# Moving two thirds of a conditioning product into the common weight stream of a hybrid decoder trunk

## The chip, the cores and the metric

The kernel runs on one core of one Trainium2 chip. The metric is the device time of one execution in microseconds (us). A core has five engines that this text names: PE (TensorE, matmuls, with its weight loads PEld), DVE (VectorE), ACT (ScalarE), POOL (GpSimd) and SP (SyncE, which here only issues DMAs). Each runs its own list of instructions in order and waits on semaphores for the others.

## The reference

All values are float32. With P = 128, D = 1024, 2048 prompt positions and 8 x 8 = 64 sample positions:

```
mod = silu(c) @ w_ada + b_ada                     # (9 conditioning rows) x 1024 x 6144
sh1, sc1, g1, sh2, sc2, g2 = split(mod, 6)
h   = x * (1 + sc1) + sh1
a_b, a_c, a_x, g_u, g_v, p_x = split(h @ w_in)    # 1024 x 2048
y_a = a_b * conv3(a_c * a_x)                      # 256 channels
y_b = g_u * (W_s @ LN(g_v) + b_s)                 # 512 channels, 128 x 128 per head and chunk
y_c = pool_map(trailing_means(p_x) - p_x)         # 256 channels
x   = LN(alpha * x + g1 * (concat(y) @ w_out))
h2  = x * (1 + sc2) + sh2
x   = LN(alpha * x + g2 * (relu(h2 @ w_up)**2 @ w_down))
```

There are 9 conditioning rows: one for the prompt, eight for the sample batch. New convolution, pooling and gating states are outputs too. The change concerns `mod`: only `sh1` and `sc1` are needed before the first projection; `g1`, `sh2`, `sc2` and `g2` are needed later.

## The kernel before, in words

**Precision.** A float32 product of large operands is three matmuls of split operands (`mm3`, lines 844 to 847): each operand is a high part of type fp32r and a low part (value minus high part). A weight slab is 128 x 1024 values (512 KB). SP loads it into one of `RAW = 2` raw buffers (`slab`), ACT copies it to the high part in one of `SLOTS = 4` slots of `w_hilo` (line 744, `hi_part`), and POOL subtracts to make the low part (line 686, `lo_part`). Slab g is loaded once the low part of slab g - 2 is made, and its high part is made once PE is done with slab g - 4. All of `w_in`, `w_out`, `w_up` and `w_down` passes through this one stream.

**Supers.** The prompt is cut in four supers of 512 positions; the fourth also carries the 64 sample positions (tiles `nt == 5`, 576 columns). For each super a mixer runs: four slabs for v (`v_slab`), then the "F phase" of twelve feature-major slabs F0 to F11 (`fm_product`, 24 matmuls each), then eight output slabs (`o_product`). The parts of F0 to F11 are, in order, c x b of the first 128 convolution channels, pool 0, u 0, pool 1, u 1, then c x b of the second half, u 2, u 3. Between them stand S (position mixing of tiles 0, 1 and of 2, 3), M (the pooling map, which waits for the pooled differences `d_ready` from DVE) and, in the first super, B (a bias table). The order is written out by hand in `mixer_stages`, once for PE and once for DVE. After the four mixers comes the MLP, 16 groups per super.

**Banks.** The F slabs of supers 1 and 2 take four PSUM banks in turn, those of the first and the fourth super two.

**The modulation product.** `w_ada` is cut in `N_ADA = 24` pieces of 256 columns (1 MB each). For a piece, SP loads the weights and the bias row (into 9 partitions), PE runs 8 plain float32 matmuls with 9 stationary columns (`ada_product`, line 857), DVE adds the bias (line 1199), PE turns the result in two transposes (`ada_turn`, line 865), DVE copies it to `modT` (lines 1208, 1210), and SP stores the row to `mod_rows`. Eight pieces (`ADA_FIRST`) stand in the opening, between the first transposes of x and the v slabs; the other sixteen stand in the F phase of the first super (`("A", u)`). `g1` and `g2` come back from `mod_rows` by a broadcast load. Two pieces share two banks, so the next product waits for DVE's copy of the last (`ada_T`).

**The opening.** The small tables, the state rows and w_s are loaded before pieces 1 and 2 and the tiles of x.

Of the kernel before, what the change touches and what calls it, by code (L numbers as in the profile page):

```python
# [38 lines left out]
MIX_SLABS = 24  # L39
SLAB_FM, SLAB_O = 4, 16  # L40
# [13 lines left out]
N_ADA = 24  # L54
ADA_COLS = 6 * D // N_ADA
ADA_FIRST = 2 * D // ADA_COLS


def ada_col(u):

    if u < ADA_FIRST:
        return (SH1 if u % 2 else SC1) * D + ADA_COLS * (u // 2)
    return ADA_COLS * u


N_PRE = 3 + 2 + 2 + 1 + 1 + 2 + 1
# [27 lines left out]
def fm_turns(nt, first):  # L94
    return 2 if nt == 5 or first else 4


def fm_bank(f, nt, first):
    return 2 * (f % 2) if nt == 5 or first else f % 4
# [53 lines left out]
def ada_pieces_after(f):  # L153
    return [ADA_FIRST + 2 * f, ADA_FIRST + 2 * f + 1] if f < 4 else [ADA_FIRST + 4 + f]


def mixer_stages(s, vector):


    nt, first = tiles_of(s), s == 0  # L160
    F = [("F", n) for n in range(N_FM)]
    S01, S23 = ("S", [0, 1], 0 if nt == 4 else 1), ("S", [2, 3], 2 if nt == 4 else 3)
    if nt == 5:
        S4 = ("S", [4], 0)
        a = [S4, ("V", 1), F[0], ("V", 1)] if vector else [F[0], S4]
        a += [F[1], F[2]] if not vector else [F[1]]
        a += [S01, ("V", 2)] + ([F[2]] if vector else []) + [S23, F[3], F[4]]
    elif vector or first:
# [16 lines left out]


def decoder_layer_kernel(nc, x_prompt, x_sample, c_prompt, c_sample, state_conv, state_pool,
# [5 lines left out]
    with ctx:  # L193
# [38 lines left out]
        hB = sb("hB", [P, 2, KD, GT + ST], F32R)  # L232
# [20 lines left out]
        siluT = sb("siluT", [P, KD * (1 + NB)])  # L253
        ln_now = (sb("mv", [P, 5, 2]), sb("rstd", [P, 5]), sb("rtmp", [P, 5]))
# [38 lines left out]
        ada_out = [sem(f"ada_out{i}") for i in range(4)]  # L293
# [12 lines left out]
        s_pret = sem("s_pret")  # L306
        bias_in = sem("bias_in")
# [101 lines left out]
        def _(sp):  # L409
            def ada_weights(u):  # L410
                if u >= 3:
                    sp.wait_ge(ada_mm, u - 2 if u < ADA_FIRST else u - 1)
# [27 lines left out]
            sp.dma_start(w_s_rows[:, :].rearrange("p (h j) -> p h j", h=HEADS),  # L440
                         w_s[0].rearrange("h i j -> i h j")).then_inc(s_pre, 16)
            sp.dma_start(htmp[0:NB * CONV_BUF, 0, 0:W_CONV],
                         state_conv[0].rearrange("b r c -> (b r) c")).then_inc(s_pre, 16)
            sp.dma_start(htmp[0:NB * POOL_BUF, 1, 0:W_POOL],
                         state_pool[0].rearrange("b r c -> (b r) c")).then_inc(s_pre, 16)
            for half in range(2):
                sp.dma_start(gate_tab[64 * half:64 * half + 64, :, :],
                             bcast(b_s[0].rearrange("(q two) i -> two q i", two=2)[half], 64)
                             ).then_inc(s_pre, 16)
            for c in range(2):  # L450
                sp.dma_start(convw[:, c, :],
                             conv_w[0, :, P * c:P * c + P].rearrange("w p -> p w")).then_inc(s_pre, 16)
            sp.dma_start(pscale[:, :], pool_scale[0].rearrange("(c p) -> p c", p=P)).then_inc(s_pre, 16)
# [1285 lines left out]
```

## Time and profile before

| | us |
|---|---|
| median of three timed runs | 2272.57 (2272.53 to 2274.78) |
| the profiled execution | 2271.71 |
| its span | 2270.0 |
| PE busy | 2190.1, 96% of the span |
| POOL busy | 984.3, 43% |
| DVE busy | 1325.3, 58% |
| mean granted clock of PE | 0.985 of full speed |

The span is what the profiler saw from the first to the last instruction; 1.7 us of the execution lie around it. In the 40 slices of the page PE is below nine tenths only in the first two and in the last. The spans of the stages are: opening 0 to 80 us, F phase of the first super 80 to 236, F phases of supers 1, 2 and 3 305 to 386, 455 to 536 and 610 to 716, MLP from 774 on.

### The profile page before, as it was taken

The page shows a single profiled execution, that of the slowest core. Times are in us where ns is not written, and L with a number is a line of the kernel's source. Part 1 is how long each engine was busy: PE and PEld are TensorE (multiplying, and loading weights), DVE is VectorE, ACT ScalarE, POOL GpSimd, SP SyncE. Part 2 cuts the span into 40 slices and gives each one's busy share as a digit, 9 for nine tenths or more (in the row PEclk, how much of TensorE's full clock was granted, in tenths as well). Part 3 has the DMA queues.
Part 4 walks back from the last instruction along what each step waited for, and adds up shares of the span by engine and source line. Part 5 has one row for each costly group of instructions (what it writes and reads, how often), then busy time and mean ns, then how long its engine had stood idle before and what let it go on. Part 6 is the DMA issues. An engine that isn't in the chain of part 4 may idle for free.

```text
span 2270.0 us, 26946 instructions
## 1 busy us (share of the span) xinstructions
PE 2190.1 (96%) x10686; PEld 1811.2 (80%) x10686; DVE 1325.3 (58%) x1970; ACT 628.0 (28%) x871; POOL 984.3 (43%) x429
## 2 busy tenths in 40 slices
PE   7989999999999999999999999999999999999995
PEld 3556787887788888888888888888888889999994
DVE  1555568587576733654386664376664466555448
ACT  1201322323212333234232333323234322222221
POOL 3312343433323344444464544465454464444454
PEclk9999999999999999999999999999999999999998
DMA  8535353352333245343333434333433322332221
GB/s 257 164 125 175 140 167 103 102 176 102 117 100 117 75 135 167 107 121 111 101 91 123 149 97 126 93 100 104 150 121 102 116 84 77 126 129 88 75 86 50
DMA packets 262832, 269.37 MB, mean 119 GB/s; under 512 B 13080, under 2 KB 220137, under 8 KB 262706
## 3 DMA queue, kind: packets, MB, share of 16 engines
q1 hardware_dynamic: 262706, 267.64, 37.3%
q8 instruction: 85, 1.39, 0.2%
q14 instruction: 41, 0.34, 0.0%
HBM read 249.78 MB, written 17.81 MB: 118 GB/s over the span
## 4 chain that ended last, share of the span: by engine, by line
PE 64%; DVE 4%; POOL 2%; DMA 1%; issue 0%; ACT 0%; DVEq 0%
PE ps L845 21%; PE ps L846 21%; PE ps L847 21%; POOL acc L711 1%; POOL w_hilo L686 1%; PE ps L978 1%; PE ps L1123 1%; PE ps L1124 1%; DMA w_raw<-in_w_up 1%; DVE xt L1607 0%; DVE htmp L1431 0%; DVE hid L1590 0%; DVE st L1233 0%; DVE hid L1593 0%; DVE xt L1635 0%
## 5 line engine op out<-in xcount | busy, mean ns | idle before, releaser
L686 POOL TENSOR_TENSOR w_hilo<-w_raw,w_hilo 128x1024 fp32r<-128x1024 f32 x352 | 910.8, 2596 | 1251.7 <-ACT w_hilo L744 1251.7
L744 ACT ACTIVATE w_hilo<-w_raw 128x1024 fp32r<-128x1024 f32 x352 | 365.4, 1055 | 1070.2 <-PE ps L847 877.1
L1666 DVE TENSOR_TENSOR acc<-acc,ps 128x512 f32<-128x512 f32 x490 | 330.3, 686 | 212.4 <-PE ps L847 204.8
L845 PE MATMUL ps<-w_hilo,hid 128*128 128x512 f32 x1024 | 399.2, 390 | 1.6 <-DVE acc L1663 1.0
L846 PE MATMUL ps<-w_hilo,hid 128*128 128x512 f32 x1024 | 398.7, 389 | 0.0
L847 PE MATMUL ps<-w_hilo,hid 128*128 128x512 f32 x1024 | 398.4, 389 | 0.0
L845 PE MATMUL ps<-hA,w_hilo 128*128 128x512 f32 (+1 forms) x992 | 373.4, 376 | 8.3 <-DVE acc L1460 4.2
L846 PE MATMUL ps<-hA,w_hilo 128*128 128x512 f32 (+1 forms) x992 | 371.1, 374 | 0.0
L847 PE MATMUL ps<-hA,w_hilo 128*128 128x512 f32 (+1 forms) x992 | 370.7, 374 | 0.0
L1590 DVE CAST hid<-htmp 128x512 fp32r<-128x512 f32 (+1 forms) x128 | 61.6, 481 | 378.9 <-ACT htmp L790 378.2
L845 PE MATMUL ps<-hB,w_hilo 128*128 128x288 f32 (+1 forms) x768 | 250.7, 326 | 0.0
L847 PE MATMUL ps<-hB,w_hilo 128*128 128x288 f32 (+1 forms) x768 | 250.4, 326 | 0.0
L846 PE MATMUL ps<-hB,w_hilo 128*128 128x288 f32 (+1 forms) x768 | 250.3, 326 | 0.0
L845 PEld LDWEIGHTS ps<-w_hilo,hid 128*128 128x128 f32 x1024 | 192.2, 188 | 44.0 <-DVE acc L1663 2.4
L847 PEld LDWEIGHTS ps<-w_hilo,hid 128*128 128x128 f32 x1024 | 192.2, 188 | 40.3
L846 PEld LDWEIGHTS ps<-w_hilo,hid 128*128 128x128 f32 x1024 | 192.2, 188 | 39.0
L845 PEld LDWEIGHTS ps<-hA,w_hilo 128*128 128x128 f32 x992 | 189.0, 191 | 40.2 <-DVE acc L1460 4.5
L847 PEld LDWEIGHTS ps<-hA,w_hilo 128*128 128x128 f32 x992 | 188.8, 190 | 31.8
L846 PEld LDWEIGHTS ps<-hA,w_hilo 128*128 128x128 f32 x992 | 189.1, 191 | 30.8
L788 ACT ACTIVATE htmp<-ps 128x512 f32<-128x512 f32 (+1 forms) x128 | 78.2, 611 | 438.4 <-PE ps L847 438.4
L845 PEld LDWEIGHTS ps<-hB,w_hilo 128*128 128x128 f32 x768 | 144.0, 188 | 10.5
L846 PEld LDWEIGHTS ps<-hB,w_hilo 128*128 128x128 f32 x768 | 144.1, 188 | 10.4
(197 smaller groups left out, 2486.7 us busy)
## 6 DMA issues: line engine op xcount, KB each, us to landing
w_raw<-in_w_up SPq DMA_DIRECT2D x128, 512.0 KB, 4.1
w_raw<-in_w_down SPq DMA_DIRECT2D x128, 512.0 KB, 3.6
w_raw<-in_w_in SPq DMA_DIRECT2D x64, 512.0 KB, 3.8
xt<-in_w_ada SPq DMA_DIRECT2D x22, 1024.0 KB
w_raw<-in_w_out SPq DMA_DIRECT2D x32, 512.0 KB, 3.7
xt<-in_x_prompt SPq DMA_DIRECT2D x16, 512.0 KB, 6.8
x_norm<-xt SPq DMA_DIRECT2D x16, 512.0 KB, 6.4
xt<-x_norm SPq DMA_DIRECT2D x16, 512.0 KB, 6.0
```

The source lines that it names most:

```text
L686: pool.tensor_tensor(W[:, g % SLOTS, 1, :], raw[:, g % RAW, :], W[:, g % SLOTS, 0, :], ALU.subtract).then_inc(lo_done, 1)
L711: pool.tensor_tensor(a, a, rows[:, G2_ROW, :], ALU.mult).then_inc(acc_gated, 1)
L744: act.activation(W[:, g % SLOTS, 0, :], raw[:, g % RAW, :], ACT.Copy).then_inc(hi_done, 1)
L788: act.activation(h, fm_view(2 * i, nt), ACT.Relu).then_inc(s_chain_act, 1)
L845: pe.matmul(out, w_hi, x_hi, start=start, stop=False)
L846: pe.matmul(out, w_hi, x_lo, start=False, stop=False)
L847: return pe.matmul(out, w_lo, x_hi, start=False, stop=stop)
L978: ins = pe.transpose(ps[:, set_banks(e, t)[k // 4], P * (k % 4):P * (k % 4) + P], src[:, P * k:P * k + P], ident[:, :])
L1123: pe.matmul(out, x, w_hi, start=start, stop=False)
L1124: return pe.matmul(out, x, w_lo, start=False, stop=stop)
L1590: signal(dve.tensor_copy(hi, x), s_hid_hi, f + 1)
L1666: dve.tensor_tensor(a, a, src, ALU.add).then_inc(d_evac, 1)
```

## The change

1. **Late slabs.** g1, sh2, sc2 and g2, one for each mixer in this order (`LATE`), no longer use pieces. Each is eight slabs of the common stream (`SLAB_A`, two k-tiles x 512 columns each), so a mixer has 32 slabs, not 24. PE multiplies `silu2` (18 stationary columns: the high parts of the 9 rows and their low parts) with the high and the low part of the slab: 4 matmuls a slab (`late_slab`).
2. **Folds.** After four late slabs DVE copies the 18 rows to `arow` (stage C), PE adds the two halves and the bias with a stacked identity in float32 (`late_turn`, stage T; one matmul for g1 and g2, four small ones for sh2 and sc2), and DVE keeps the result (stage K). g1 and g2 are stored to `mod_rows`.
3. **Order.** The late slabs stand from F5 on: F5 A A F6 A A F7 T M F8 A A M F9 A A F10 T F11. On DVE C0 stands behind the work of F6, C1 behind that of F9.
4. **First super.** Its F slabs now take four banks in turn; B stands directly behind F0, its halves in two banks.
5. **Opening.** c, the bias columns, pieces 0 and 1 and the four tiles of x are loaded first (all in `front`, which lies over hB), then the rest in order of use; the bias is added in turned form from `modb`; the low parts of slabs 0 to 3 are made before POOL's preparation of the tables; the small tables are loaded between slabs 4 and 7.
6. **Residual loads.** The four loads of x for the residual (2 MB) follow slab 21 of 32, where they followed slab 13 of 24 (in the first super: they stood before slab 21 of 24).

```diff
-MIX_SLABS = 24
-SLAB_FM, SLAB_O = 4, 16
+MIX_SLABS = 32
+SLAB_F = [4, 5, 6, 7, 8, 9, 12, 15, 16, 19, 22, 23]
+SLAB_A = [10, 11, 13, 14, 17, 18, 20, 21]
+SLAB_O = 24
-N_ADA = 24
-ADA_COLS = 6 * D // N_ADA
+ADA_COLS = 256
+N_ADA = 2 * D // ADA_COLS
+LATE = [G1, SH2, SC2, G2]
+BOTH = 2 * (1 + NB)
...
-    a += [F[5], F[6], F[7], ("M", 0), F[8], ("M", 1)] + F[9:]
...
+    A = [("A", i) for i in range(8)]
+    if vector:
+        a += [F[5], F[6], ("C", 0), F[7], ("K", 0), ("M", 0), F[8], ("M", 1), F[9], ("C", 1), F[10], ("K", 1), F[11]]
+    else:
+        a += [F[5], A[0], A[1], F[6], A[2], A[3], F[7], ("T", 0), ("M", 0), F[8], A[4], A[5], ("M", 1), F[9],
+              A[6], A[7], F[10], ("T", 1), F[11]]
...
-            lo_part(0)
-            lo_part(1)
+            for g in range(4):
+                lo_part(g)
...
+            def late_slab(s, nt, i):
+                g, bank = MIX_SLABS * s + SLAB_A[i], 6 + i // 4
+                pe.wait_ge(lo_done, g + 1)
...
+                for kk in range(2):
+                    k = 2 * (i % 4) + kk
+                    for part in range(2):
+                        ins = pe.matmul(ps[0:BOTH, bank, :], silu2[:, k, :],
+                                        W[:, g % SLOTS, part, HALF * kk:HALF * kk + HALF],
+                                        start=(k == 0 and part == 0), stop=(k == KD - 1 and part == 1))
+                ins.then_inc(slab_used, 1)
+            def late_turn(u):
+                pe.wait_ge(late_copied, u + 1)
+                pe.wait_ge(late_in, 16 * (u + 1))
...
+                if late_row(u // 2):
+                    ins = pe.matmul(ps[0:1 + NB, bank, :], stack[0:r, :], arow[0:r, :], start=True, stop=True)
+                else:
+                    for q in range(4):
+                        ins = pe.matmul(ps[:, bank, (1 + NB) * q:(1 + NB) * (q + 1)], arow[0:r, P * q:P * q + P],
+                                        stack[0:r, :], start=True, stop=True)
...
+            def late_copy(s, u):
+                dve.wait_ge(slab_used, MIX_SLABS * s + SLAB_A[4 * (u % 2) + 3] + 1)
...
+                signal(dve.tensor_copy(arow[0:BOTH, :], ps[0:BOTH, 6 + u % 2, :]), late_copied, u + 1)
...
                     elif stage[0] == "B":
...
-                            pe.wait_ge(fm_evac, 1)
-                            if half:
-                                pe.wait_ge(bias_kept, 1)
-                            ins = sgu_product(ps[:, 0, :], spl[:, 1, :, :], wsT, P, half)
+                            if half == 0:
+                                pe.wait_ge(fm_evac, 1)
+                            ins = sgu_product(ps[:, 3 * half, :], spl[:, 1, :, :], wsT, P, half)
...
-                    if n == 13:
-                        sp.wait_ge(n_stored, 64 * s)
+                    if n == SLAB_A[7]:
+                        if late_row(s):
+                            late_store(2 * s)
+                        if s:
+                            sp.wait_ge(n_stored, 64 * s)
+                        else:
+                            sp.wait_ge(xs_split, 1)
                         load_residual(s)
```

On PE, in the first super between F5 and F6, before (silu is the conditioning, hA the split input, w_hilo the split slab):

```order
L847 MATMUL ps<-hA,w_hilo 128x512
L857 MATMUL ps<-xt,siluT 9x256 x8
L865 MATMUL ps<-ident,gs 128x9 x2
L845 MATMUL ps<-hA,w_hilo 128x512
L846 MATMUL ps<-hA,w_hilo 128x512
```

and now:

```order
L874 MATMUL ps<-hA,w_hilo 128x512
L1014 MATMUL ps<-w_hilo,silu 18x512 x8
L872 MATMUL ps<-hA,w_hilo 128x512
L873 MATMUL ps<-hA,w_hilo 128x512
L874 MATMUL ps<-hA,w_hilo 128x512
```

The piece of 256 columns (8 program matmuls) and its two transposes have become two slabs of 4 matmuls each.

On DVE, in super 1 from the end of pool 1 (F5) over u 1 (F6) to the work of F7 and M0 (spl holds the pooled differences, hB the mixer's output), before:

```order
L1253 CAST spl<-htmp 128x512
L1254 TENSOR_TENSOR spl<-htmp,spl 128x512
L1460 TENSOR_TENSOR acc<-ps,acc 128x512
L1253 CAST hB<-acc 128x512
L1254 TENSOR_TENSOR hB<-acc,hB 128x512
L1377 COPY htmp<-ps 128x512
L1453 TENSOR_SCALAR acc<-ps,pscale 128x512
```

and now (htmp with 18 rows is `arow`):

```order
L1347 CAST spl<-htmp 128x512
L1348 TENSOR_TENSOR spl<-htmp,spl 128x512
L1554 TENSOR_TENSOR acc<-ps,acc 128x512
L1347 CAST hB<-acc 128x512
L1348 TENSOR_TENSOR hB<-acc,hB 128x512
L1293 COPY htmp<-ps 18x512
L1471 COPY htmp<-ps 128x512
L1303 COPY modT<-ps 128x36
```

C0 (line 1293), for which PE's fold T0 waits, stands behind all of DVE's work for F5 and F6.

On SP, in super 1 from the stores of x_norm to the first output slab, before:

```order
L528 DMA x_norm<-xt 128x1024 x4
L500 DMA w_raw<-in_w_in 128x8x128 x4
L514 DMA xt<-in_x_prompt 128x1024 x4
L500 DMA w_raw<-in_w_in 128x8x128 x2
L500 DMA w_raw<-in_w_out 128x2x512
```

and now:

```order
L500 DMA x_norm<-xt 128x1024 x4
L517 DMA htmp<-in_b_ada 1x512
L472 DMA w_raw<-in_w_ada 128x2x512 x2
L472 DMA w_raw<-in_w_in 128x8x128
L472 DMA w_raw<-in_w_ada 128x2x512 x2
L472 DMA w_raw<-in_w_in 128x8x128 x2
L472 DMA w_raw<-in_w_ada 128x2x512 x2
L472 DMA w_raw<-in_w_in 128x8x128
L472 DMA w_raw<-in_w_ada 128x2x512 x2
L486 DMA xt<-in_x_prompt 128x1024 x4
L472 DMA w_raw<-in_w_in 128x8x128
```

Twelve slabs stand between the stores and the residual loads where four stood, and the residual loads now stand directly ahead of slab 22.

## Rows read from the trace of the kernel before

**Rows 1.** The page: busy us (share of the span) x instructions of each engine
```profile
PE 2190.1 (96%) x10686; PEld 1811.2 (80%) x10686; DVE 1325.3 (58%) x1970; ACT 628.0 (28%) x871; POOL 984.3 (43%) x429
```

**Rows 2.** Stages: length; busy us of PE, PEld, DVE, ACT, POOL; PE clock, DMA share, GB/s
```profile
80.00:236.00 156.00, 142.59 (x647) 88.20 (x646) 82.26 (x163) 16.41 (x17) 34.21 (x14) 0.97 0.47 149
305.00:386.00 81.00, 75.33 (x346) 62.50 (x345) 67.11 (x111) 15.33 (x17) 29.44 (x12) 0.96 0.43 144
610.00:716.00 106.00, 93.70 (x651) 92.27 (x651) 84.23 (x163) 15.45 (x17) 29.55 (x12) 0.92 0.34 116
```

**Rows 3.** PE from 80 to 236 us, by form: busy us, mean ns; idle before, releaser
```profile
L857 PE MATMUL ps<-xt,siluT 128*9 128x256 f32 x256 | 62.0, 399 | 9.2 <-DVE modT L1210 9.2
L865 PE MATMUL ps<-ident,gs 9*128 9x9 f32 x32 | 4.6, 213 | 0.4 <-DVE gs L1199 0.4
```

**Rows 4.** PE in order of time, two pieces: start, us, what [idle before <-releaser]
```profile
141.31 3.62 PE L857 MATMUL ps<-xt,siluT 128*9 128x256 f32 x16
...
150.24 6.36 PE L857 MATMUL ps<-xt,siluT 128*9 128x256 f32 x16 [5.10 <-DVE modT L1210]
```

**Rows 5.** PE in order of time, super 1: starts of F5, F6, F8, M1, F9
```profile
339.44 0.40 PE L845 MATMUL ps<-hA,w_hilo 128*128 128x512 f32 x1
...
344.91 0.39 PE L845 MATMUL ps<-hA,w_hilo 128*128 128x512 f32 x1
...
356.47 0.39 PE L845 MATMUL ps<-hA,w_hilo 128*128 128x512 f32 x1
...
366.24 0.79 PE L845 MATMUL ps<-spl,pwT 128*128 128x512 f32 x1 [4.17 <-DVE spl L1254]
...
367.69 0.63 PE L845 MATMUL ps<-hA,w_hilo 128*128 128x512 f32 x1
```

**Rows 6.** PE's waits, 283 to 774 us: us in total, times, longest
```profile
PE ps L845 <- DVE spl L1254: 11.9, 3, 4.2
...
PE ps L845 <- DVE acc L1460: 4.2, 1, 4.2
```

**Rows 7.** DVE in order of time, super 1: pool 1, then u 1
```profile
355.19 0.17 DVE L1410 COPY acc<-pcarry 128x15 f32<-128x15 f32 x1
...
363.45 2.74 DVE L1254 TENSOR_TENSOR spl<-htmp,spl 128x512 fp32r<-128x512 f32 x1
...
367.41 0.69 DVE L1254 TENSOR_TENSOR hB<-acc,hB 128x512 fp32r<-128x512 f32 x1
```

**Rows 8.** POOL in order of time, the same stretch: low parts of slabs
```profile
346.31 2.77 POOL L686 TENSOR_TENSOR w_hilo<-w_raw,w_hilo 128x1024 fp32r<-128x1024 f32 x1 [5.89 <-ACT w_hilo L744]
...
357.19 2.71 POOL L686 TENSOR_TENSOR w_hilo<-w_raw,w_hilo 128x1024 fp32r<-128x1024 f32 x1 [3.04 <-ACT w_hilo L744]
363.30 2.34 POOL L686 TENSOR_TENSOR w_hilo<-w_raw,w_hilo 128x1024 fp32r<-128x1024 f32 x1 [3.40 <-ACT w_hilo L744]
```

**Rows 9.** Loads of w_raw, 270 to 420 us
```profile
DMA to landing us min/median/max: 3.4/3.8/4.5
```

**Rows 10.** ACT in order of time: a slab's high part
```profile
404.86 1.06 ACT L744 ACTIVATE w_hilo<-w_raw 128x1024 fp32r<-128x1024 f32 x1 [2.54 <-PE ps L847]
```

**Rows 11.** SP in order of time, first super: residual loads and the slab behind them
```profile
235.17 1.78 SPq L514 DMA_DIRECT2D xt<-in_x_prompt  x4
...
237.60 0.45 SPq L500 DMA_DIRECT2D w_raw<-in_w_out  x1
```

**Rows 12.** Loads of w_raw, 230 to 262 us
```profile
DMA to landing us min/median/max: 3.5/4.3/9.3
```

**Rows 13.** PE, first super: start of F0
```profile
79.94 0.39 PE L845 MATMUL ps<-hA,w_hilo 128*128 128x512 f32 x1
```

**Rows 14.** DVE, first super: its copy of F0
```profile
89.66 0.69 DVE L1377 COPY htmp<-ps 128x512 f32<-128x512 f32 x1
```

**Rows 15.** PE in the opening: first piece, first transposes of x
```profile
7.40 6.10 PE L857 MATMUL ps<-xt,siluT 128*9 128x256 f32 x16 [3.18 <-DMA gs<-in_b_ada]
...
28.47 0.33 PE L914 MATMUL ps<-ident,acc 128*128 128x128 f32 x1 [3.08 <-DMA xs<-in_x_prompt]
```

More of the change, by code:

```diff
@@ L91, in chunks, with fm_turns, fm_bank @@
     return [(0, GT)] if nt == 4 else [(0, (GT + ST) // 2), ((GT + ST) // 2, GT + ST)]
[L94 to L99, printed above, removed]
+def fm_turns(nt):
+    return 4 if nt == 4 else 2
+def fm_bank(f, nt):
+    return f % 4 if nt == 4 else 2 * (f % 2)
 def v_order(nt):
@@ L167, in mixer_stages @@
         a += [S01, ("V", 2)] + ([F[2]] if vector else []) + [S23, F[3], F[4]]
-    elif vector or first:
+    elif first:
+        a = [F[0], ("B", 0), F[1], S01, ("V", 2), F[2], S23, F[3], F[4]]
+    elif vector:
         a = [F[0], F[1], S01, ("V", 2), F[2], S23, F[3], F[4]]
@@ L292, in decoder_layer_kernel @@
         ada_T = sem("ada_T")
-        ada_out = [sem(f"ada_out{i}") for i in range(4)]
+        late_in = sem("late_in")
+        late_copied = sem("late_copied")
+        late_fold = sem("late_fold")
+        late_kept = sem("late_kept")
+        late_out = sem("late_out")
+        s_silu2 = sem("s_silu2")
+        s_modb = sem("s_modb")
+        st_pre = sem("st_pre")
+        xs_in = sem("xs_in")
         x0_tr = sem("x0_tr")
@@ L446, in _ @@
[L446 to L453, printed above, removed]
@@ new lines, in _ @@
+            ada_weights(1)
+            for t in range(4):
+                sp.dma_start(x0_tile[t], x_prompt[0, P * t:P * t + P, :]).then_inc(x0_loaded, 16)
+            slab(0, free=False)
+            ada_weights(2)
+            ada_weights(3)
+            slab(1, free=False)
+            sp.dma_start(w_s_rows.rearrange("p (h j) -> p h j", h=HEADS),
+                         w_s[0].rearrange("h i j -> i h j")).then_inc(w_s_in, 16)
+            ada_weights(4)
+            slab(2)
+            ada_weights(5)
@@ new lines, in _ @@
+            slab(4)
+            sp.dma_start(g1row[:, 0:W_GMLP], bcast(sgu_b[0], P)).then_inc(bias_in, 16)
+            for half in range(2):
+                sp.dma_start(gate_tab[64 * half:64 * half + 64, :, :],
+                             bcast(b_s[0].rearrange("(q two) i -> two q i", two=2)[half], 64)
+                             ).then_inc(s_pre, 16)
+            slab(5)
+            for c in range(2):
+                sp.dma_start(convw[:, c, :],
+                             conv_w[0, :, P * c:P * c + P].rearrange("w p -> p w")).then_inc(s_pre, 16)
@@ L720, in _ @@
             gate_after = [up_slab(min(MLP_GROUPS * (s + 1) + 1, ALL_GROUPS - 1)) + 1 for s in range(SUPERS)]
-            for g in range(2, N_SLABS):
+            for g in range(4, N_SLABS):
                 lo_part(g)
@@ L990, in mixer @@
                         f = stage[1]
-                        turns = fm_turns(nt, first)
+                        turns = fm_turns(nt)
                         if f >= turns:
@@ new lines, in w_s_turned @@
+            def w_s_turned():
+                dve.wait_ge(s_prepe, 1)
+                dve.wait_ge(s_prep, 1)
+                for half in range(2):
+                    ins = dve.tensor_copy(prep[:, 1, HALF * half:HALF * half + HALF], ps[:, 2 * half, :])
+                    if half:
+                        ins.then_inc(s_pret, 1)
+                    else:
+                        do(ins)
+            ada_copy(0)
+            for n in range(4):
+                ada_copy(2 * n + 1)
+                ada_turned(2 * n)
+                ada_turned(2 * n + 1)
```

427 lines of the change are left out of this document (222 added, 205 removed).

## The prediction

> **What bounds the kernel now.** I read the page's busy table, then the stages, then PE's instruction groups and waits in the F phases, then PE, DVE, POOL and SP in order of time there. PE is busy for 96% of the span, POOL for 43%, DVE for 58% [rows 1]. So PE's own work and PE's waits make the time. The averages hide one thing: in the F phase of super 1 DVE is busy 67.1 of 81.0 us [rows 2], and PE waits there for DVE, 4.17 us before M1 [rows 5]; the same wait makes most of the 11.9 us in three waits of the later mixers, and 4.2 us in the last super [rows 6]. In the F phase DVE runs well behind PE and is nearly as long as PE. The MLP, two thirds of the time, is not touched.
>
> **What goes.** In the first super PE runs 16 pieces. They show as 256 rows, since a float32 matmul shows as two, 62.0 us, with 4.6 us of transposes and 9.2 us of waits for DVE's copies [rows 3]. One wait of 5.10 us is followed by a piece of 6.36 us where others take 3.62 [rows 4]: after such a wait PE runs at half pace (1.2 GHz for 2.4) for some us, which costs 2.7 us here. In super 1 M1's matmuls after the 4.17 us wait show 0.79 us and F9's first 0.63 where others show 0.39 [rows 5]; I put that loss at 2.3, a little under the 2.7 of the longer wait, and 1.7 in the last super.
>
> **What comes on PE.** A slab of 24 matmuls takes 344.91 - 339.44 = 5.47 us, 0.228 each [rows 5]. A late slab is 4 matmuls over 512 columns; the trace has none with 18 stationary columns. I take 0.228 too (9 or 128 stationary columns move at one pace per pass in it): 0.91 a slab, 7.3 for eight, 29.2 for 32. From below it could be nothing cheaper than half (0.45 a slab), from above the float32 pace of rows 4, 3.62/8 = 0.45 for 256 columns, so 3.6 a slab. The folds are float32: 512 columns cost twice a piece's matmul, 0.9 us; the four small ones some 0.6. Eight folds: about 6 us.
> The Trainium skill, "TensorE: Matmul & The Clock Gate", back-to-back issue gap, gives about 131 ns per matmul of 512 columns in a stream. By it the 32 late slabs would cost an estimated 17 us. Rows 5 show 0.228 us, so I stay with 29.2.
>
> **The supply.** A late slab uses PE for 0.91 us but costs the stream as much as any other. With two raw buffers one slab needs 3.8 us of load [rows 9], 1.06 of high part [rows 10] and 2.4 of low part [rows 8], 7.3 us for two slabs in flight, so 3.7 us per slab. F slabs use 5.47. Where F5 ends, four slabs are ready or nearly so; the pattern F A A uses three slabs in 7.3 us and needs 11. Step by step from the end of F5 (344.9, call it 0): low parts of slabs 13, 14, 15, 16 end at 3.7, 6.3, 11.2, 13.8. PE gets to F7 (slab 15) at 9.2 and waits 2 us. Slab 22 stands behind 2 MB of residual loads: at 237.60 such a slab landed 9.3 us after its issue [rows 11, 12], so it would be ready at 41.4, where PE would come at 34 if nothing else held it: a wait of 7.4.
>
> **DVE holds it first.** T0 waits for C0, and C0 stands behind pool 1 and u 1. In the trace DVE starts pool 1 at 355.19, 10.3 us after the end of F5, and ends u 1 at 367.41 + 0.69 = 368.1 [rows 7], 23.2 after it. PE reaches T0 at 1.8 + 5.5 + 1.8 + 2 + 5.5 = 16.6. So T0 waits 23.2 + 0.7 (the copy) - 16.6 = 7.3 us even if DVE is no slower than now. But it is slower: the subtraction of line 1254 takes 2.74 us at 363.45, under POOL's low part of 363.30, and 0.69 at 367.41 without one [rows 7, 8]. DVE's operations on SBUF stand still while POOL works, 2.05 us here. From 344.9 to 368.1 there are four low parts (346.31, one more, 357.19, 363.30) [rows 8]; with the packed stream there are seven (slabs 13 to 19). Three more at 2.05 put C0 at about 30 and the wait at 13. Lower bound 7.3, upper 15. I take 12, nearer to the collisions that rows show each time. Then the clock falls: 2.5 us.
> The rule that speaks against this change: the Trainium skill, "GPSIMD Engine Reference", specifications, says that GpSimd's SBUF interface is shared with VectorE and contended by instructions with two SBUF inputs or in a two-port mode. By that rule, the trace agrees (2.74 against 0.69).
>
> Behind a T0 that late, slab 20 can be made only after F8 (slot of slab 16), and slab 22 only after slab 20: 20.6 us after C0, where PE comes at 19: 1.8 us of wait. The residual loads are hidden then.
>
> **The sum** (against the profiled execution, 2271.7; the median of the runs is 0.9 above).
> Supers 1 and 2: PE's F phase of 81.0 [rows 2] loses the M1 wait, 4.2, and its clock, 2.3; gains late slabs 7.3, folds 1.5, F7 2, T0 12, clock 2.5, F10 1.8: +20.6 each. Bounds: +15 (T0 7.3, but then slab 22 makes PE wait again) and +24.
> Super 3, F slabs longer by an eighth: 106.0 loses 4.2 and 1.7 of clock, gains 7.3, 1.8, 1, 12, 2.5, 0.5: +19; the sparser stream makes it +17. Bounds +9 and +20.
> First super: the work left is 12 x 5.47 = 65.6, S and its short waits 7.5 (what super 1's 81.0 leaves after its slabs, M 1.4, and the 6.5 above), M 1.4, B 2.0, late slabs 7.3, folds 1.8: 85.6. Waits: the pieces covered DVE's norm; its copy of F0 starts at 89.66, 9.7 after F0 starts at 79.94 [rows 13, 14], and B now stands directly behind F0's 5.5, so it waits 5. S01 then stands directly behind F1 and waits some 3 for DVE's convolution. F7 2, T0 11, F10 2, and three falls of the clock 7.5: 30.5. Total 116 against 156.0 [rows 2]: -40. Bounds -49 and -36.
> Opening: PE starts the first piece at 7.40 and the transposes of x only at 28.47, both behind loads, and small tables stand between them [rows 15]. With large loads alone in front I put x at 16 and the pieces never more than 2 us late; PE then needs 8 x 3.6 + 4 x 5.5 + 6 and ends near 71.5 for 79.94: -8. Bounds -12 (no wait for pieces 2 and 3) and -3 (each of the three loads waited for there comes 1.5 to 2 us later).
> Costed at nothing: C1, K0, K1, the small stores and bias loads. DVE's slack from F8 on covers them; without it, 0.7 each.
> Sum: -40 + 2 x 20.6 + 17 - 8 = +10; with T0 at 13 in all, +14. I take +12: 2284 for the profiled execution, 2285 as a median.
>
> **Rivals.**
> A, faster: POOL's packed low parts do not lengthen DVE's chain (they fall on PSUM reads, which rows do not show slowed), T0 waits 7, and slab 22 behind the residual loads is the second wait: -49 + 2 x 15 + 9 - 8 = -18: 2254. For it: 7.3 is all that present times give. Against it: rows 7. The sign turns where the four T0 waits average 9 us rather than 12.
> B, slower: both bounds together, T0 15, and slab 22 late as well: -36 + 48 + 20 - 3 = +29: 2301. For it: each lock loss delays the next low part too.
> C, no saving, the change doesn't do what it says: 18 columns with split slabs run at the float32 pace. 32 x 2.7 = 86 more, 40 of it in T0's waits: 2331. Against it: fp32r slabs on the moving side run at 0.228 in the v slabs.
> D, even: gain in the first super and loss in the others cancel: 2272.
>
> **How the numbers follow.** Forecast (2277 to 2296) 0.47, A 0.27, B 0.15, C 0.02, D 0.09. A measurement tells 0.2%, 4.5 us, from no change. Of A 0.23 are faster and 0.04 the same; of D 0.08 the same and 0.01 slower; B and C are slower; of the forecast's mechanism 0.44 are slower, and 0.03 fall under its range, 0.02 faster and 0.01 the same, by an opening or a first super better than taken. Faster 0.25, same 0.13, slower 0.62. The range is 2256 to 2301; the forecast's own is 2277 to 2296.
>
> **What would show it.** Right: T0's first matmul in each super idle about 12 us behind DVE's copy of 18 rows; C0 about 30 us after F5's end; DVE's SBUF operations from F5 to C0 at 2 to 3 us each; M1 without a wait; the first super's F phase near 116, the others near 102, 102 and 123; F0 starting near 71.5. Wrong: T0 idle 7 us or less with F10 idle over 5 (A); late matmuls above 0.3 us (C); an opening that ends after 77; a second wait in F10 over 4 beside a long T0 (B).

## The result: 1.07% slower, and the profile after

The changed kernel takes 2297.8 us (median of 5 runs, 2293.59 to 2299.83), the kernel before 2272.76 in the same comparison (5 runs). The ratio is 1.0107, 95% interval 1.0096 to 1.0119. The forecast was 2285. The profiled execution took 2293.59 us, 21.9 more than the 2271.7 of before; it is the lowest of the five, and where the other 3 us of the median stand no profile shows.

The page of the profile after, to be held against [rows 1]:
```profile
span 2291.9 us, 26787 instructions
...
PE 2176.9 (95%) x10567; PEld 1812.8 (79%) x10567; DVE 1373.9 (60%) x1959; ACT 660.5 (29%) x903; POOL 1068.1 (47%) x465
```
PE is busy 13 us less than before and the span is 22 us longer: PE's waits grew by 35 us. DVE is busy 49 us more and POOL 84.

The stages, with the columns of [rows 2]: the F phases of supers 0 to 3, and the MLP with the tail.
```profile
75.00:194.00 119.00, 95.08 (x392) 72.67 (x391) 89.14 (x132) 23.89 (x25) 51.74 (x21) 0.89 0.37 115
263.00:367.00 104.00, 86.92 (x391) 68.61 (x390) 81.39 (x115) 22.59 (x23) 47.61 (x19) 0.92 0.46 146
436.00:543.00 107.00, 89.84 (x395) 70.60 (x394) 83.73 (x118) 23.64 (x24) 50.77 (x20) 0.90 0.45 145
617.00:735.00 118.00, 101.96 (x686) 93.84 (x685) 92.63 (x167) 22.58 (x23) 44.64 (x19) 0.94 0.41 131
793.00:2291.00 1498.00, 1468.66 (x7158) 1247.45 (x7156) 847.43 (x1119) 453.47 (x612) 729.13 (x278) 0.99 0.35 109
```
In super 1 DVE is busy 81 of 104 us where it was 67 of 81, and POOL 48 where it was 29. PE's granted clock, 0.96 before, is 0.92: 2.4 GHz for most of the time and 1.2 in stretches behind waits.

PE's waits up to 800 us, to be held against [rows 6] and the 9.2 us of [rows 3]:
```profile
PE ps L1030 <- DVE htmp L1293: 22.9, 2, 11.6
PE ps L872 <- POOL w_hilo L711: 16.1, 8, 3.1
PE ps L1027 <- DVE htmp L1293: 12.4, 2, 7.9
PE ps L872 <- DVE acc L1418: 10.0, 7, 5.5
PE ps L872 <- DVE htmp L1471: 6.3, 1, 6.3
```
L1030 and L1027 are the two forms of the fold T0, and L1293 is DVE's copy C0. The four waits at T0 make 35.3 us, the largest new item. POOL's line is F7, F10 and short ones; the last two lines are S01 and B, mostly in the first super.

PE in order of time in super 1, with the columns of [rows 5] (F5 ends where the first late pair starts):
```profile
303.65 2.00 PE L1014 MATMUL ps<-w_hilo,silu 128*18 128x512 f32 x8
310.97 2.03 PE L1014 MATMUL ps<-w_hilo,silu 128*18 128x512 f32 x8
315.44 0.77 PE L872 MATMUL ps<-hA,w_hilo 128*128 128x512 f32 x1 [2.44 <-POOL w_hilo L711]
...
334.06 1.87 PE L1030 MATMUL ps<-stack,htmp 19*128 19x9 f32 x8 [11.57 <-DVE htmp L1293]
335.86 0.79 PE L872 MATMUL ps<-spl,pwT 128*128 128x512 f32 x1
...
337.31 0.63 PE L872 MATMUL ps<-hA,w_hilo 128*128 128x512 f32 x1
...
355.10 0.47 PE L872 MATMUL ps<-hA,w_hilo 128*128 128x512 f32 x1 [1.57 <-POOL w_hilo L711]
```
In order: A0 A1, A2 A3, F7 behind a wait, T0 behind 11.57 us, M0 and F8 still at 0.63 to 0.79 a matmul where 0.39 is full pace, and F10. A late pair costs 1.85 us (F6 starts at 305.50), 0.93 a slab.

DVE and POOL in the same stretch, against [rows 7, 8]: a step of pool 1 under a low part, the ends of pool 1 and of u 1, and C0; then POOL's first and seventh low part.
```profile
323.69 2.71 DVE L1523 TENSOR_TENSOR acc<-acc 128x512 f32<-128x512 f32 x1
328.67 2.71 DVE L1348 TENSOR_TENSOR spl<-htmp,spl 128x512 fp32r<-128x512 f32 x1
332.60 0.69 DVE L1348 TENSOR_TENSOR hB<-acc,hB 128x512 fp32r<-128x512 f32 x1
333.32 0.68 DVE L1293 COPY htmp<-ps 18x512 f32<-18x512 f32 x1
```
```profile
305.05 2.78 POOL L711 TENSOR_TENSOR w_hilo<-w_raw,w_hilo 128x1024 fp32r<-128x1024 f32 x1 [5.88 <-ACT w_hilo L769]
...
328.27 2.55 POOL L711 TENSOR_TENSOR w_hilo<-w_raw,w_hilo 128x1024 fp32r<-128x1024 f32 x1 [2.42 <-ACT w_hilo L769]
```
C0 starts 333.32 - 303.65 = 29.7 us after F5's end, where u 1 ended 23.2 after it before. That is the forecast step.

In the last super T0 waits less. F5 ends at 675.54, C0 starts 23.7 us behind it, with six low parts between them for the seven of super 1. PE, then DVE:
```profile
700.00 1.26 PE L1027 MATMUL ps<-htmp,stack 19*9 19x512 f32 x2 [4.58 <-DVE htmp L1293]
```
```profile
699.26 0.68 DVE L1293 COPY htmp<-ps 18x512 f32<-18x512 f32 x1
```

Where the 21.9 us are, by the starts and ends of the phases (the last line is read from PE at the start of the MLP):

| | before | after | change | forecast |
|---|---|---|---|---|
| F0 starts | 79.94 | 75.38 | -4.6 | -8 |
| F phase, super 0 | 155.6 | 118.9 | -36.7 | -40 |
| super 1 | 81.1 | 104.1 | +23.0 | +20.6 |
| super 2 | 81.2 | 106.6 | +25.4 | +20.6 |
| super 3 | 105.6 | 117.9 | +12.3 | +17 |
| MLP and tail | 1496.1 | 1498.7 | +2.6 | 0 |

In the first super T0 waits 7.85 us, C0 24.6 us behind F5's end (157.69 - 133.13). Seven low parts stand there too, but DVE is less far behind PE. PE's T0, then DVE's first operation for pool 0 in super 0 and in super 1:
```profile
158.42 1.87 PE L1027 MATMUL ps<-htmp,stack 19*9 19x512 f32 x2 [7.85 <-DVE htmp L1293]
```
```profile
124.47 1.62 DVE L1504 COPY acc<-pcarry 128x15 f32<-128x15 f32 x1
303.12 0.18 DVE L1504 COPY acc<-pcarry 128x15 f32<-128x15 f32 x1
```
That is 8.7 us ahead of F5's end in super 0 and 0.5 in super 1 (F5 ends at 303.65).

### The profile page after: what moved, and what is told of

Read it like the earlier page. It is cut to its first block, busy times and chain, and to the rows that moved or that the text cites. A ratio compares the mean times of both kernels' runs of the same rounds, so it can differ in the third digit from the quotient of the medians.

```text
span 2291.9 us, 26787 instructions
## 1 busy us (share of the span) xinstructions
PE 2176.9 (95%) x10567; PEld 1812.8 (79%) x10567; DVE 1373.9 (60%) x1959; ACT 660.5 (29%) x903; POOL 1068.1 (47%) x465
## 4 chain that ended last, share of the span: by engine, by line
PE 63%; DVE 5%; POOL 2%; DMA 1%; issue 0%; ACT 0%; DVEq 0%; ACTq 0%
PE ps L872 21%; PE ps L873 20%; PE ps L874 20%; DVE xt L1711 1%; POOL acc L736 1%; POOL w_hilo L711 1%; PE ps L1049 1%; PE ps L1198 1%; PE ps L1199 1%; DVE hid L1697 0%; DMA w_raw<-in_w_up 0%; DVE hid L1694 0%; DVE htmp L1525 0%; DVE st L1327 0%; DVE acc L1519 0%
## 5 line engine op out<-in xcount | busy, mean ns | idle before, releaser
L711 POOL TENSOR_TENSOR w_hilo<-w_raw,w_hilo 128x1024 fp32r<-128x1024 f32 x384 | 993.9, 2597 | 1189.2 <-ACT w_hilo L769 1189.1
L769 ACT ACTIVATE w_hilo<-w_raw 128x1024 fp32r<-128x1024 f32 x384 | 398.4, 1054 | 1065.0 <-PE ps L874 715.8
```

The source lines that it names most:

```text
L711: pool.tensor_tensor(W[:, g % SLOTS, 1, :], raw[:, g % RAW, :], W[:, g % SLOTS, 0, :], ALU.subtract).then_inc(lo_done, 1)
L769: act.activation(W[:, g % SLOTS, 0, :], raw[:, g % RAW, :], ACT.Copy).then_inc(hi_done, 1)
```

## The experiments

All are timed against the kernel before on the same chip, 4 to 10 runs each. Each edit is to the changed kernel, unless the text says otherwise. This table has F0's start, the four F phases and the start of the MLP of each profiled run, and the median with the ratio to before.

| | F0 | F phases | MLP | us | ratio (95%) |
|---|---|---|---|---|---|
| after | 75.4 | 118.9 104.1 106.6 117.9 | 793.2 | 2297.8 | 1.0107 (1.0096 to 1.0119) |
| C0 early | 75.7 | 116.8 94.0 94.2 119.9 | 771.0 | 2273.5 | 1.0007 (0.9998 to 1.0016) |
| T0 late | 75.8 | 122.8 95.9 100.4 129.6 | 795.0 | 2293.4 | 1.0088 (1.0070 to 1.0106) |
| small low parts | 75.9 | 108.9 93.9 93.0 114.6 | 756.7 | 2257.9 | 0.9942 (0.9925 to 0.9959) |
| residual late | 76.4 | 117.5 106.7 105.5 119.4 | 800.6 | 2301.1 | 1.0132 (1.0116 to 1.0148) |
| C0 early, residual late | 75.4 | 112.9 98.4 98.9 112.7 | 770.8 | 2274.1 | 1.0008 (0.9999 to 1.0018) |
| and C1 early | 75.2 | 112.2 90.5 90.4 112.9 | 765.3 | 2261.8 | 0.9940 (0.9926 to 0.9953) |
| B behind F1 | 75.4 | 108.1 105.3 105.6 119.1 | 784.0 | 2285.7 | 1.0058 (1.0045 to 1.0070) |
| opening | 73.8 | 117.2 107.9 105.5 116.4 | 791.2 | 2294.5 | 1.0094 (1.0080 to 1.0107) |
| all of these | 72.5 | 102.9 92.6 94.6 113.0 | 749.9 | 2248.0 | 0.9889 (0.9876 to 0.9903) |
| and the store | 72.1 | 102.4 92.3 94.5 113.1 | 746.7 | 2248.8 | 0.9890 (0.9875 to 0.9906) |
| and late slabs spread | 72.4 | 97.8 93.5 94.1 120.4 | 749.8 | 2251.9 | 0.9909 (0.9893 to 0.9924) |

### Is it the place of C0? Its copy early
```diff
-        a += [F[5], F[6], ("C", 0), F[7], ("K", 0), ("M", 0), F[8], ("M", 1), F[9], ("C", 1), F[10], ("K", 1), F[11]]
+        a += [F[5], F[6]]
+        a.insert(-1 if nt == 5 else -2, ("C", 0))
+        a += [F[7], ("K", 0), ("M", 0), F[8], ("M", 1), F[9], ("C", 1), F[10], ("K", 1), F[11]]
```


> Only VectorE's order changes: its copy of the first 18-row half (C0) stands ahead of pool 1 in supers 0 to 2, and behind pool 1 but ahead of u 1 in the last. Theory (T0 waits because C0 stands behind 13 to 30 us of VectorE's chain): the four waits at T0 of 7.9, 11.6, 11.3 and 4.6 us go nearly to 0, and the clock's loss behind them (1.5 each) with them, about -40. F8 then comes sooner, and slab 22, behind 2 MB of residual loads, is late: F10's wait grows from 1.9 to some 8 in supers 0 to 2, +18. Sum about -22: 2275. Rival (the packed stream is the limit, T0 only the first to show it): PE waits as long at F8, M1 or F9; 2292 to 2299.

Measured 2273.5: 24 us less than the changed kernel, at the expected figure. In super 1 T0 stands at 319.11 directly behind F7 with no wait. The wait that comes instead in super 0 is F10's, the slab behind the residual loads (PE in order of time):
```profile
178.49 0.77 PE L874 MATMUL ps<-hA,w_hilo 128*128 128x512 f32 x1 [9.64 <-POOL w_hilo L713]
```
In the last super F10 waits 6.05. In super 1 it is M1, 3.42 us behind pool 1 at 331.77. The place of one copy of 0.68 us is worth the whole net loss against before.

### Is it DVE held by POOL? Small low parts
```diff
+                n = P if g < MLP0 and g % MIX_SLABS in SLAB_A else D
-                pool.tensor_tensor(W[:, g % SLOTS, 1, :], raw[:, g % RAW, :], W[:, g % SLOTS, 0, :],
+                pool.tensor_tensor(W[:, g % SLOTS, 1, 0:n], raw[:, g % RAW, 0:n], W[:, g % SLOTS, 0, 0:n],
```


> Leaves out seven eighths of the low part of the 32 late slabs: GpSimd's subtraction for them is 128x128 for 128x1024 (PE still multiplies all of it, with old numbers in the rest). Theory (each low part holds VectorE's SBUF operations for 2.05 us): C0 in super 1 ends about 24 us after F5's end and not 30.4, so T0 waits some 5 for 11.6; F7's waits of 2.4 go too. Supers 0 to 2: -9 each, the last -4, with clock about -30: 2268. Rival (GpSimd's work does not lengthen VectorE's chain): T0's waits stay within 1 us of 11.6 plus what F7 gives back, total -2 to -6: 2292 to 2296.

Measured 2257.9, 40 us less than the changed kernel, more than expected. Its page:
```profile
PE 2170.8 (96%) x10567; PEld 1809.7 (80%) x10567; DVE 1309.6 (58%) x1959; ACT 661.1 (29%) x903; POOL 1004.8 (45%) x465
```
DVE has the same 1959 instructions and not one of them was changed, and it is busy 1373.9 - 1309.6 = 64.3 us less: 2.0 us for each of the 32 low parts. POOL is busy 63.3 us less. That the two agree this closely proves little: in the other runs of this section, whose low parts are whole, DVE is busy 1362.3 to 1375.5 us, so that a low part is worth 1.6 to 2.1. In super 1 F5 ends at 294.16, and on DVE
```profile
313.89 0.68 DVE L1294 COPY htmp<-ps 18x512 f32<-18x512 f32 x1
```
C0 stands 19.7 us behind it and not 29.7: five times 2.0, and two whole low parts are left there where seven stood. T0 waits 4.73. Not all of the 40 us is DVE's: the slabs come sooner too, and F7 waits 1.10, 0.70 and 0.78 us in supers 0 to 2 where it waited 2.4. The rule of the Trainium skill, "GPSIMD Engine Reference", specifications (an SBUF interface shared with VectorE), is borne out by this, with its price beside it.

### Are the residual loads hidden? They alone late
```diff
-                        load_residual(s)
...
+                    if SLAB_F[11] <= n < SLAB_F[11] + 4:
+                        load_residual(s, [n - SLAB_F[11]])
```


> Only SyncE's order changes: the four residual tiles are loaded one by one behind slabs 23 to 26 instead of all together between slabs 21 and 22. Theory (hidden behind the long T0): F10's waits of 1.9 stay, since slab 22 waits for slab 20 and that for F8's slot; no change within 3 us, 2295 to 2300. Rival (slab 22 is late by its load): F10's waits go, -2 and some clock in three supers, about -9: 2289.

Measured 2301.1, 3 more than the changed kernel, with intervals that touch. F10 still waits 1.9 to 2.1 us in supers 0 to 2. Beside a long T0 the loads cost nothing where they stand, as forecast; late, they seem to cost a few us in the output phases (the MLP starts 7.4 us later, of which F0 and the F phases make 2.6).

### With T0 out of the way: both edits, then C1 too


> Both edits, VectorE's early C0 and the residual tiles behind slabs 23 to 26. Theory: the waits at T0 go and slab 22 does not take their place: -40 in all, 2258; F phases near 105, 91, 93 and 112. Rival (stream packed two late slabs to one F slab is the limit): no more than 3 us better than the early C0 alone.

Measured 2274.1, the same as with C0 early alone. The theory's 2258 was wrong and the rival's figure came, but not by its mechanism. F10's long wait in super 0 falls from 9.6 to 3.8 (112.9 for 116.8), but in super 1 the next fold, T1, takes its place (in the last super 7 us are gained, in supers 1 and 2 4.4 and 4.7 lost). PE, then DVE:
```profile
345.98 0.38 PE L1033 MATMUL ps<-stack,htmp 19*128 19x9 f32 x1 [4.78 <-DVE htmp L1296]
```
```profile
345.24 0.68 DVE L1296 COPY htmp<-ps 18x512 f32<-18x512 f32 x1
```
DVE runs without a gap from F5's end at 297.70 to this copy C1. Its order has C1 behind pool out 1 and the b copy, so the fold once more stands where PE meets the end of DVE's chain. The next run moves C1 ahead of both:
```diff
-        a += [F[7], ("K", 0), ("M", 0), F[8], ("M", 1), F[9], ("C", 1), F[10], ("K", 1), F[11]]
+        a += [F[7], ("K", 0), ("M", 0), F[8], ("C", 1), ("M", 1), F[9], F[10], ("K", 1), F[11]]
```


> Early C0 and late residual tiles as in the run before, and C1 ahead of pool out 1 and the b copy on VectorE. Theory (VectorE is now the longer chain, and each fold is a point where PE meets its end): T1's waits of 4.8 and 4.0 in supers 1 and 2 go, with 1.5 of clock each; part of it comes back as waits for hB ahead of the output products. Total -7: 2267. Rival (VectorE busy without a gap to the end of the mixer, so that whatever is moved PE waits for its end): within 2 us of 2274.

Measured 2261.8, 12 less, where 7 were expected. T1 stands at 340.22 behind F10 with no wait and supers 1 and 2 take 90.5. This is faster than before by 0.6%.

### The same on PE's side: T0 behind M1
```diff
-        a += [F[5], F[6], ("C", 0), F[7], ("K", 0), ("M", 0), F[8], ("M", 1), F[9], ("C", 1), F[10], ("K", 1), F[11]]
+        a += [F[5], F[6], ("C", 0), F[7], ("M", 0), F[8], ("M", 1), ("K", 0), F[9], ("C", 1), F[10], ("K", 1), F[11]]
     else:
-        a += [F[5], A[0], A[1], F[6], A[2], A[3], F[7], ("T", 0), ("M", 0), F[8], A[4], A[5], ("M", 1), F[9],
+        a += [F[5], A[0], A[1], F[6], A[2], A[3], F[7], ("M", 0), F[8], A[4], A[5], ("M", 1), ("T", 0), F[9],
```


> The changed kernel, and only PE's place for the first fold: T0 stands behind M1 (and VectorE's K0 behind its pool out 1), C0 stays behind u 1. Theory (the 35 us at T0 are a matter of where PE meets VectorE, not of the copy being early): as with the early copy, F8 no longer waits for C0, T0's waits fall under 1, M1 waits some 3 for u 1's chain, F10's wait grows behind the residual loads: 2274, within 4 us of the early copy's 2273.5. Rival (the early copy helped by shortening something else, K0 or the store): 2285 or more.

Measured 2293.4, 19 over the expected figure. In supers 1 and 2, where no store stands, it does most of what was expected, 95.9 and 100.4 (T0 still waits 2.3). In supers 0 and 3, where the half is a gate half and SP stores it, F10 is late, by 16.57 and 9.73 us. PE in super 0, then SP in order of time:
```profile
183.92 0.76 PE L872 MATMUL ps<-hA,w_hilo 128*128 128x512 f32 x1 [16.57 <-POOL w_hilo L711]
```
```profile
158.33 0.37 SPq L472 DMA_DIRECT2D w_raw<-in_w_ada  x1
169.67 0.30 SPq L522 DMA_DIRECT2D mod_rows<-htmp  x1
170.01 1.77 SPq L486 DMA_DIRECT2D xt<-in_x_prompt  x4
171.83 0.52 SPq L472 DMA_DIRECT2D w_raw<-in_w_in  x1
```
SP stands at the store of K0, 11 us behind slab 21, and the slabs stand behind it. The error was mine: K0 moved along with T0, and what SP has queued behind the store was not counted. The total lies with the rival (2285 or more), and by what the rival named, the store. So this run does not say which side of the meeting is better to move; it says that slabs queued behind a store wait as long as the store does.

### The first super: B behind F1 and F2 ahead of S01
On PE alone:
```diff
         a = [F[0], ("B", 0), F[1], S01, ("V", 2), F[2], S23, F[3], F[4]]
+        if not vector:
+            a = [F[0], F[1], ("B", 0), F[2], S01, S23, F[3], F[4]]
```


> The changed kernel with one edit: in the first super PE runs F0, F1, B, F2, S01 for F0, B, F1, S01, F2. Theory (B and the second half of S01 stand too soon behind VectorE, 6.3 and 5.5 us): both waits and two falls of the clock go on PE, 12 us up to F5's end; but VectorE's own chain gains only the 4.3 us by which F1 comes earlier, and T0 waits for that chain, so T0's wait of 7.9 grows by some 7 and the total gains 4 to 5: 2293. Rival 1 (PE's waits are worth their length): -12: 2286. Rival 2 (nothing moves on VectorE): 2298.

Measured 2285.7, 12 less than the changed kernel: the first rival, not my theory. B waits 1.78 for 6.30 and S01's second half 0.94 for 5.49; S23 gets a wait of 3.60 that it did not have. T0's wait did not grow, it fell to 5.53. DVE's copy C0 there:
```profile
147.41 0.68 DVE L1295 COPY htmp<-ps 18x512 f32<-18x512 f32 x1
```
C0 came at 157.69 in the changed kernel, so DVE's chain gained 10.3 us, not 4.3. DVE had itself been waiting for PE, 4.55 and 2.52 us at F1's and F2's copies, and PE for DVE: in this stretch the two waited for each other in turn, and one order removed most of both.

### The opening
```diff
+            for c in range(2):
+                sp.dma_start(convw[:, c, :],
...
+            sp.dma_start(lnT[:, 1, :], ln1_b[0].rearrange("(k p) -> p k", p=P)).then_inc(s_pre, 16)
             sp.wait_ge(s_prep, 1)
...
                     state_transposes()
-                v_slab(0, n)
+                    v_slab(0, 2)
+                if n != 2:
+                    v_slab(0, n)
```
The six loads of convw, pscale, sgu_gT and lnT stood behind slabs 5 and 6.

> The changed kernel with the opening alone edited: v slab 2 stands behind the last small transposes, directly ahead of v slab 3, and the small tables (convw, pscale, sgu_g, ln1) are loaded before pool_w's corners. Theory (the opening's missing 3.4 us are the 2 us of short waits ahead of v slab 3 and the 2.5 us by which it runs at half pace behind them): v slab 3 takes 5.7 for 8.2, F0 starts at 71.5 for 75.4, all behind it moves along: 2294. Rival (the lost clock is only put off, into the transposes and v slab 2): F0 at 74 to 75, total within 1 us of 2298.

Measured 2294.5, 3.3 less than the changed kernel with intervals that touch (1.0080 to 1.0107 against 1.0096 to 1.0119); F0 starts at 73.79, not quite half-way to the 71.5 expected: in part the theory, in part its rival. In the changed kernel v slab 3 starts behind 0.84 us of waiting, after two other short waits, at 0.77 a matmul, and the granted clock is 0.54 to 73.0. Two windows of the changed kernel, with the columns of [rows 2]:
```profile
67.40:73.00 5.60, 5.60 (x14) 4.40 (x15) 5.43 (x6) 0.00 (x0) 4.54 (x2) 0.54 0.44 94
73.00:75.40 2.40, 2.40 (x13) 1.93 (x12) 1.22 (x4) 1.06 (x1) 0.29 (x1) 1.00 0.75 113
```
With the edit, from the start of v slab 2:
```profile
61.50:67.00 5.50, 5.50 (x21) 4.43 (x20) 5.36 (x5) 1.23 (x2) 5.38 (x3) 0.74 0.00 0
67.00:74.00 7.00, 7.00 (x32) 5.82 (x31) 6.48 (x9) 1.06 (x1) 4.51 (x3) 1.00 0.54 147
```
The wait for hA is covered; the low clock is shorter and not gone.

### All edits together, the store, and the late slabs spread


> All edits together: early C0 and C1, residual tiles behind slabs 23 to 26, B behind F1, and the opening. If they add up: 2267 - 8 for the first super (its T0 no longer stands in the way) - 4 for the opening: 2255, 0.8% faster than the kernel before. Rival (first super bound by VectorE like the others): 2263 to 2266.

Measured 2248.0: ratio 0.9889 to before and 2.2% under the changed kernel, below the 2255 that adding up gave. Its page, for [rows 1]:
```profile
PE 2166.9 (96%) x10567; PEld 1805.2 (80%) x10567; DVE 1370.2 (61%) x1959; ACT 661.5 (29%) x903; POOL 1066.7 (47%) x465
```
The same work as in the changed kernel on every engine; only the order differs.

The store behind slab 22 (an edit to the run before):
```diff
                     if n == SLAB_A[7]:
-                        if late_row(s):
-                            late_store(2 * s)
...
                     if n == SLAB_F[10]:
+                        if late_row(s):
+                            late_store(2 * s)
```


> All edits, and the store of the first gate half behind slab 22 instead of ahead of it. Theory (in supers 0 and 3 SyncE holds slab 22 until K0, 2.4 us after its raw buffer is free at 150.5): F10's wait in the first super falls from 4.5 to 2.1, total 2245, 2.5 below the run without it. Rival (slab 22 late by the low parts alone): 2248.

Measured 2248.8, no difference: F10's wait in super 0 falls from 4.53 to 1.52 us, and T1 gets one of 2.90 behind C1 (PE in order of time):
```profile
157.67 0.47 PE L877 MATMUL ps<-hA,w_hilo 128*128 128x512 f32 x1 [1.52 <-POOL w_hilo L716]
166.29 1.02 PE L1034 MATMUL ps<-htmp,stack 19*9 19x512 f32 x2 [2.90 <-DVE htmp L1300]
```

And the late slabs spread, again on top; T0 moves behind F8 with them, and in the first super C0 behind pool 1:
```diff
-SLAB_F = [4, 5, 6, 7, 8, 9, 12, 15, 16, 19, 22, 23]
+SLAB_F = [4, 5, 6, 7, 8, 9, 11, 14, 16, 19, 22, 23]
-SLAB_A = [10, 11, 13, 14, 17, 18, 20, 21]
+SLAB_A = [10, 12, 13, 15, 17, 18, 20, 21]
...
-        a.insert(-1 if nt == 5 else -2, ("C", 0))
+        a.insert(-1 if nt == 5 or first else -2, ("C", 0))
...
-        a += [F[5], A[0], A[1], F[6], A[2], A[3], F[7], ("T", 0), ("M", 0), F[8], A[4], A[5], ("M", 1), F[9],
+        a += [F[5], A[0], F[6], A[1], A[2], F[7], A[3], ("M", 0), F[8], ("T", 0), A[4], A[5], ("M", 1), F[9],
```


> All edits, the store too, and the late slabs spread: F5 A0 F6 A1 A2 F7 A3 M0 F8 T0 A4 A5 M1 for F5 A0 A1 F6 A2 A3 F7 T0 M0 F8 A4 A5 M1. Theory (two raw buffers make one slab in about 3.65 us; F7 as the 15th slab after F5 needs 11.6 us of making and PE is there at 9.2; as the 14th it needs 7.9): F7's four waits of 2 to 3 us go, and the half pace behind one or two of them: -10 against the run with the store, 2235. Rival (the waits only move to slab 15, 18 or to M1, since VectorE's chain is as long as PE's here): 2243 to 2246.

Measured 2251.9: the rival's mechanism, and slower than its 2243 to 2246. F7's waits go, as worked out, and super 0 takes 97.8; but M1 waits 7.08 in super 1, and super 3 takes 120.4 with waits for DVE's copies (PE, M1 of super 1 and a wait in super 3):
```profile
311.57 0.80 PE L877 MATMUL ps<-spl,pwT 128*128 128x512 f32 x1 [7.08 <-DVE spl L1355]
...
650.87 0.61 PE L877 MATMUL ps<-hA,w_hilo 128*128 128x288 f32 x1 [4.46 <-DVE acc L1561]
```
In these stretches PE waits for DVE's chain. The late slabs and T0 were moved together; which of the two cost the last super its 7 us was not tested.

## Why the prediction was right, and where its sizes were not

Direction, mechanism and range (2256 to 2301) held; the point was 13 us low, and 2297.8 lies 1.8 over the forecast's own range (2277 to 2296). The change was forecast as 12 us and is 25. That it came no further out is partly luck: the four T0 waits were put at 47 us in all and are 35.3, while the clock, the opening, S01 and the MLP were put too low, and the errors cancel in part.

- **T0 waits some 12 us for C0, since three more low parts lengthen DVE's chain.** Right in supers 1 and 2: 11.57 and 11.30, C0 29.7 us behind F5's end for a forecast of about 30, seven low parts counted. Shown by two runs: C0 early removes the wait, small low parts shorten DVE's chain by 10.0 us. In super 0 it is 7.85 for 11 and in super 3 4.58 for 12: there the term was wrong, since super 1's timing was carried over to both. In super 0 DVE starts pool 0 8.7 us ahead of F5's end and not 0.5, PE having waited for it at B and S01; in super 3 F slabs of 6.4 us leave six low parts ahead of C0 and not seven. Rival A's condition (T0 7) was met in these two supers and not in the other two; the average of the four is 8.8, just under the 9 at which I had put the sign's turn.
- **So why was it slower all the same?** The term that was most too low is the clock. I took one fall of 2.5 us a super. In super 1 F7 behind its short wait takes 6.9 for 5.47, and T0, M0 and F8 behind the long one lose 2.2: 3.6 in all. In super 2 F7 loses 1.7, T0, M0 and F8 2.8, and F10, which waits 1.9, another 1.6: 6.1 in all. In the first super F1, B, S01, F2, M0, F8 and F10 run at half pace at least in part, some 10 us for 7.5. Of the seven waits of 1.6 to 3.1 us at F7 and F10, four were followed by a loss of 1.4 to 1.7 us in clock.
- **First super -40.** Measured -36.7: B 6.3 for 5, S01 5.5 for 3, F7 2.4 for 2, T0 7.85 for 11, F10 1.9 for 2: the waits' sum of 24 was forecast as 23, since T0's error cancels those of B and S01; the rest is the clock.
- **Opening -8.** Measured -4.6. The forecast's sum does not close as it is written: 56.8 us from x at 16 end at 72.8, and 71.5 needs the first two pieces ahead of x. They ran there: x is in place at 16.48 as taken, and the pieces run as worked out. The term left out three short waits ahead of v slab 3 and its half pace, 8.2 us for 5.7.
- **Late slabs 0.91, folds 0.9 and 0.6.** Measured 0.93 and about 1.0 for either form. Eighteen stationary columns pass at the pace of 128; rival C is out.
- **F7 2, F10 1.8, residual hidden.** 2.4 to 3.1, 1.6 to 1.9 (0.34 in super 3), and hidden: the run with them late is no faster.
- **M1 without a wait.** Right.
- **The MLP untouched.** It is, but it takes 2.6 us more: PE waits 2.48 us at 1886.66 for an accumulator copy, behind DVE subtractions of 2.94 and 2.38 us that fell under low parts. PE there:
```profile
1886.66 0.50 PE L872 MATMUL ps<-w_hilo,hid 128*128 128x512 f32 x1 [2.48 <-DVE acc L1767]
```
  Four other runs of the changed order (C0 early, small low parts, B behind F1, all of these) have a wait of 2.2 us there, so it is no matter of one run; why it was not there before was not tested.

Not settled: which waits bring the clock down and which do not. F7's 2.4 us in super 1 is followed by half pace in the changed kernel and by full pace in the run with C0 early (5.6 us behind a wait of 2.33).

## What to carry to other kernels

A small operation whose result the longest engine waits for must not stand behind a long chain of a second engine that is nearly as long: ask for each such copy what is queued ahead of it, and put it where its input is ready. When work is moved into a denser stream, count what each of its stages takes from neighbours (here 2.0 us of VectorE for each low part of GpSimd), and add to each short wait the clock that may go with it (here 1.4 to 1.7 us behind four waits of seven). When two engines wait for each other in turn, one change of order can give more than either wait (here 10.8 us of the F phase, for waits of 6.3 and 5.5).

## What the runs showed of the hardware

- A GpSimd subtraction over 128x1024 costs VectorE about 2.0 us of standing still, measured with seven eighths of 32 of them left out (64.3 us, or 1.6 to 2.1 for each by the spread between runs) and in single rows (2.71 us for 0.69). It also holds operations with one SBUF input: a 128x512 cast took 2.24 us for 0.43 and a copy of 15 columns 2.22 for 0.17 in super 1 of the changed kernel:
```profile
313.34 2.24 DVE L1347 CAST hB<-acc 128x512 fp32r<-128x512 f32 x1
...
316.34 2.22 DVE L1504 COPY acc<-pcarry 128x15 f32<-128x15 f32 x1
```
  The forms that read PSUM were not held. DVE up to 800 us, by form: busy us, mean ns:
```profile
L1348 DVE TENSOR_TENSOR hB<-acc,hB 128x512 fp32r<-128x512 f32 x24 | 29.3, 1222 | 0.8
L1348 DVE TENSOR_TENSOR hA<-ps,hA 128x512 fp32r<-128x512 f32 x32 | 22.1, 692 | 1.1
L1347 DVE CAST hA<-ps 128x512 fp32r<-128x512 f32 x32 | 22.1, 691 | 45.5 <-ACT ps L793 45.0
L1347 DVE CAST hB<-acc 128x512 fp32r<-128x512 f32 x24 | 21.7, 906 | 0.8
...
L1504 DVE COPY acc<-pcarry 128x15 f32<-128x15 f32 x8 | 6.9, 868 | 2.8 <-PE ps L874 2.4
```
  The forms from PSUM have a mean equal to their undisturbed 0.69; the same subtraction from SBUF has 1.22 for 0.69. DVE's commonest operation, which reads one operand from PSUM, has a mean of 0.69 too in the MLP, where POOL is busy 729 of 1498 us:
```profile
L1770 DVE TENSOR_TENSOR acc<-acc,ps 128x512 f32<-128x512 f32 x490 | 330.3, 686 | 212.4 <-PE ps L874 204.7
```
  The Trainium skill, "GPSIMD Engine Reference", specifications, names two SBUF inputs or a two-port mode; whether the cast and the copy run in such a mode no run here shows.
- A float32 fold of 19 rows over 512 columns and four folds of 9 columns take the same 1.0 us.
